# Attention scores from stacked upper and lower parts instead of full float32 products, the mask written by VectorE, and branch B loaded by thirds

## The reference, cut to what matters

```python
xn = rmsnorm(x, g_in);  h = xn @ w_in            # 5648 columns, split into dq dk dv dg gq gk gv gg ga mg
s = einsum('bqhmd,bkhmd->bhmqk', q, k) * DK**-0.5 # 4 heads, 2 maps m, DK = 64
s = where(key_chunk <= q_chunk, s, -inf)          # chunks of 64 frames; the sample group has no mask
p = softmax(s);  a = p[:, :, 0] - lam * p[:, :, 1]
oa = rmsnorm(a @ v) * (1 - lam_init) * silu(da_gate)
ob = rmsnorm(gla(gq, gk, gv, log_a)) * silu(gla_gate)
mixed = sigmoid(g_a) * (oa @ w_branch_a) + sigmoid(g_b) * (ob @ w_branch_b)
y = rmsnorm(x + mixed @ w_out)
```

## Time and profile before

| | |
|---|---|
| median of 3 runs (lowest to highest) | 948.97 us (947.03 to 949.14) |
| profiled execution, its own time | 948.3 us |
| its span, first to last instruction | 946.5 us |
| mean granted TensorE clock | 0.996 |
| PE / PEld / DVE / ACT / POOL busy | 96% / 88% / 51% / 38% / 13% |
| first attention scores, last attention scores | 401.4 us, 757.7 us |

### The profile page before, as it was taken

The page is one execution under the profiler, slowest core; times in us unless marked ns, Lnnn a source line. Parts: engine busy times, 40 slices in busy tenths (PEclk is TensorE's granted clock), DMA queues, the critical chain, the costliest instruction groups (busy, mean ns, idle before and its releaser), DMA issues. The chain is left out here.

```text
span 946.5 us, 16619 instructions
## 1 busy us (share of the span) xinstructions
PE 910.5 (96%) x6648; PEld 831.3 (88%) x6648; DVE 485.8 (51%) x1098; ACT 364.3 (38%) x878; POOL 122.6 (13%) x210
## 2 busy tenths in 40 slices
PE   5899999999999999999999999999998999999997
PEld 4699999989999999999889899898997989988884
DVE  5623377741216776244643464455447676991223
ACT  6645354422335444134443353335334332430010
POOL 2001133210102222000000000000001103540000
PEclk9999999999999999999999999999999999999999
DMA  8022012213110213151032202121123325541222
GB/s 274 2 58 58 23 46 63 76 46 99 45 45 24 68 37 96 52 193 46 24 137 74 74 1 66 54 75 46 46 91 116 91 69 177 175 165 45 89 89 78
DMA packets 85903, 74.11 MB, mean 78 GB/s; under 512 B 4730, under 2 KB 78148, under 8 KB 85572
## 3 DMA queue, kind: packets, MB, share of 16 engines
q1 hardware_dynamic: 85828, 73.06, 25.4%
HBM read 53.32 MB, written 19.73 MB: 77 GB/s over the span
## 5 line engine op out<-in xcount | busy, mean ns | idle before, releaser
L1420 PE MATMUL proj_bank<-x_hi,w_hi 128*128 128x352 f32 x1056 | 350.9, 332 | 2.5 <-DVE w_lo L627 2.5
L1422 PE MATMUL proj_bank<-x_hi,w_lo 128*128 128x352 f32 x1056 | 340.2, 322 | 0.0
L1421 PE MATMUL proj_bank<-x_lo,w_hi 128*128 128x352 f32 x1056 | 339.6, 322 | 0.0
L1420 PEld LDWEIGHTS proj_bank<-x_hi,w_hi 128*128 128x128 f32 x1056 | 199.1, 189 | 4.8 <-DVE w_lo L627 2.8
L1421 PEld LDWEIGHTS proj_bank<-x_lo,w_hi 128*128 128x128 f32 x1056 | 199.6, 189 | 0.0
L1422 PEld LDWEIGHTS proj_bank<-x_hi,w_lo 128*128 128x128 f32 x1056 | 198.9, 188 | 0.0
L627 DVE TENSOR_TENSOR w_lo<-w_raw,w_hi 128x1024 fp32r<-128x1024 f32 x49 | 59.9, 1223 | 69.8 <-ACT w_hi L623 69.8
L994 ACT ACTIVATE probs<-score_banks,softmax_stats 128x128 f32<-128x128 f32 (+8 forms) x72 | 51.2, 713 | 78.1 <-DVE softmax_stats L1336 69.3
L1062 POOL TENSOR_TENSOR stats<-stats,minus_half 128x1 f32<-128x1 f32 (+1 forms) x36 | 22.4, 622 | 371.0 <-DVE stats L1369 371.0
L1047 POOL TENSOR_TENSOR decays<-log_decay 128x128 f32<-128x128 f32 (+1 forms) x122 | 47.6, 425 | 157.7 <-ACT log_decay L931 157.7
L623 ACT ACTIVATE w_hi<-w_raw 128x1024 fp32r<-128x1024 f32 (+1 forms) x53 | 55.1, 1039 | 17.2 <-PE proj_bank L1422 14.5
(11 more groups left out here) (186 smaller groups left out, 1403.3 us busy)
## 6 DMA issues: line engine op xcount, KB each, us to landing
w_raw<-in_w_in SPq DMA_DIRECT2D x44, 512.0 KB, 4.6
merge_tanh_scratch<-feature_stage SPq DMA_DIRECT2D x16, 528.0 KB, 3.1
feature_stage<-merge_tanh_scratch SPq DMA_DIRECT2D x10, 528.0 KB, 3.6
x_rows<-in_x_prompt SPq DMA_DIRECT2D x8, 512.0 KB, 6.5
w_raw<-in_w_out SPq DMA_DIRECT2D x8, 512.0 KB, 4.5
branch_out<-in_x_prompt SPq DMA_DIRECT2D x8, 512.0 KB, 3.7
out<-branch_out SPq DMA_DIRECT2D x8, 512.0 KB, 2.6
tokens_stage<-merge_tanh_scratch SPq DMA_DIRECT2D x6, 528.0 KB, 3.7
```

Source lines behind the costliest of these rows:

```text
L1420: nc.tensor.matmul(out, wh, xh, start=first, stop=False)
L1421: nc.tensor.matmul(out, wh, xl, start=False, stop=False)
L1422: return nc.tensor.matmul(out, wl, xh, start=False, stop=last)
```

## The change

Scores: a key is stored stacked along the contraction. For map m the 128 partitions of `K[:, m, :]` hold the rounded upper part of the key in the map's own 64 partitions and the lower part in the other 64. The stationary operand `QD` has four 128-column planes per step: for each map the upper part of the query twice (both halves of the partitions), and the lower part in the map's own half with zeros in the other. Two fp32r matmuls over all 128 rows then give (q_hi·k_hi + q_hi·k_lo) + q_lo·k_hi. POOL makes both operands: `ks` stacks a third of the keys of a head, `kc` the cached 256, `qd` the queries of the next step; each POOL instruction waits for the one before (`alone`). The mask product goes; DVE overwrites the masked 64 x 64 corner of the scores with -1e30 before the maximum. `dk` units now pass through `FT`, the feature stages, as `dv` does. `OBS` goes: the last tile's x_lo products of a third come first (`ulo`), and branch B's third is then loaded from DRAM straight into BLB and split in place.

```diff
@@ stage_list
-        stages.append(("unit", t, th, 0))
+        if t < len(tiles) - 1:
+            stages.append(("unit", t, th, 0))
+        else:
+            for n in ((0, 1), (), (2,))[th]:
+                stages.append(("ulo", t, n))
+                stages.append(("obload", n))
...
+        if kind == "dk" and i:
+            keys.append(("ks", i, th))
+        elif kind == "dk":
+            stages.append(("ks", i, th))
...
+        if n == 0:
+            stages.append(("qd", 0, 0))
@@ step
         if now:
             stages.append(("aS",) + now)
+        if at_step(s + 1):
+            stages.append(("qd",) + at_step(s + 1))
...
         if two:
             stages.append(("aQ",) + two)
+        stages.extend(keys)
+        keys.clear()
+        if now and now[1] == 1:
+            stages.append(("kc", now[0]))
...
-        if s == NTT:
-            stages.append(("obload",))
@@ SP
                 elif kind == "obload":
-                    sp.wait_ge(s_obst, 16)
-                    sp.dma_start(t_["OBS"]..., ob_dram).then_inc(s_obld, 16)
+                    th = st[1]
...
+                    sp.wait_ge(s_xldone, th + 1)
+                    sp.dma_start(BLB[:, :, cols].bitcast(F), ob_dram...[:, :, cols]).then_inc(s_obld[th], 16)
@@ SP, cload of head h
-                        filled(sp, ("cache", h - 1))
+                        sp.wait_ge(s_kc, h)
@@ GpSimd
+            def alone(ins):
+                alone_no[0] += 1
+                ins.then_inc(s_pwork, 1)
+                pool.wait_ge(s_pwork, alone_no[0])
+            def stack_keys(h, cols, src, s_done):
+                K = t_["K"][h % 2]
+                for m in range(2):
+                    r, other = slice(64 * m, 64 * m + 64), slice(64 - 64 * m, P - 64 * m)
+                    alone(nc.gpsimd.tensor_copy(K[r, m, cols], src[r, :]))
+                    last = nc.gpsimd.tensor_tensor(K[other, m, cols], src[r, :], K[r, m, cols].bitcast(F), ALU.subtract)
+                    if m == 0:
+                        alone(last)
+                last.then_inc(s_done, 1)
...
+                elif st[0] == "qd":
...
+                    if s >= 2:
+                        pool.wait_ge(s_sc, 2 * (s - 1))
...
+                    for m in range(2):
+                        r, other = slice(64 * m, 64 * m + 64), slice(64 - 64 * m, P - 64 * m)
+                        alone(nc.gpsimd.tensor_copy(QD[r, 2 * m, 0:n], Q[r, tok(i)]))
+                        alone(nc.gpsimd.tensor_copy(QD[other, 2 * m, 0:n], Q[r, tok(i)]))
+                        last = nc.gpsimd.tensor_tensor(QD[r, 2 * m + 1, 0:n], Q[r, tok(i)], QD[r, 2 * m, 0:n].bitcast(F),
+                                                       ALU.subtract)
+                        if m == 0:
+                            alone(last)
+                    last.then_inc(s_qd, 1)
@@ VectorE, aS
+                        if i < TT:
+                            w = nk - 64
+                            link(nc.vector.memset(SC[0:64, 2 * m + w // 512, w % 512:w % 512 + 64], BIG))
                         link(nc.vector.reduce_max(...))
@@ TensorE, aS
-                        pe.wait_ge(s_uout, units_done(ft_at["dk", h]))
+                        pe.wait_ge(s_ks, 3 * (h + 1))
...
+                    pe.wait_ge(s_qd, s + 1)
+                    for m in range(2):
+                        if s:
+                            pe.wait_ge(s_ex, 2 * s - 1 + m)
+                        for b in range(-(-nk // 512)):
+                            keys = K[:, m, c0 + 512 * b:c0 + 512 * b + w]
+                            nc.tensor.matmul(out, QD[:, 2 * m, 0:nq], keys, start=True, stop=False)
+                            last = nc.tensor.matmul(out, QD[:, 2 * m + 1, 0:nq], keys, start=False, stop=True)
+                        last.then_inc(s_sc, 1)
```

More of the change, by code:

```diff
@@ L124, in stage_list @@
     stages = []
-    later, branch, carried = [], [], []
+    later, branch, carried, keys = [], [], [], []
     def whole(kind, i):
@@ L315, in hybrid_kernel @@
     NP_ = len(tiles)
-    ft_tiles = [t for t, (k, _, _) in enumerate(tiles) if k not in ("ga", "gk", "gq", "dq", "dk")]
+    ft_tiles = [t for t, (k, _, _) in enumerate(tiles) if k not in ("ga", "gk", "gq", "dq")]
     ft_no = {t: n for n, t in enumerate(ft_tiles)}
@@ L429, in attention @@
             low = dict(
-                GATE=[al(f"da_gate{s}", [P, T]) for s in range(2)], Q1=al("da_q1", [P, T]), K1=al("da_k1", [P, KC]),
+                QD=[al(f"q_stacked{s}", [P, 4, P], R) for s in range(2)],
+                GATE=[al(f"da_gate{s}", [P, T]) for s in range(2)], Q1=al("da_q1", [P, T]), K1=al("k_stacked1", [P, 2, KC], R),
                 V1=al("da_v1", [P, NTT + 2, DV]),
@@ L530, in hybrid_kernel @@
         s_lame = sem("lambda_exp")
-        s_obld = sem("gla_branch_loaded")
+        s_obld = [sem(f"gla_branch_loaded{th}") for th in range(3)]
         s_bh = sem("gla_branch_hi")
@@ L545, in hybrid_kernel @@
         s_gconst = sem("gla_consts_loaded")
-        s_mrld = sem("chunk_mask_loaded")
+        s_pwork = sem("pool_chain")
+        s_ks = sem("k_stacked")
+        s_kc = sem("cache_k_stacked")
+        s_qd = sem("q_stacked")
+        s_xldone = sem("x_lo_thirds_used")
         s_gfin = sem("final_gain_loaded")
@@ L853, in _ @@
                         freed(act, ("aO", i - 2, NTT - 1))
-                    if th == 0 and tk in ("dq", "dk") and i >= 2:
-                        act.wait_ge(s_sc, 2 * NTT * (i - 1))
+                    if th == 0 and tk == "dq" and i >= 2:
+                        act.wait_ge(s_qd, NTT * (i - 1))
                     act.wait_ge(s_unit, u + 1)
@@ L1458, in _ @@
                             pe.wait_ge(s_uout, u - 1)
-                    for k in range(KD_ // 2 * st[3], KD_ // 2 * (st[3] + 1)):
+                    for k in range(KD_ // 2 * st[3] if t < NP_ - 1 else 0, KD_ // 2 * (st[3] + 1)):
+                        if t == NP_ - 1:
+                            nc.tensor.matmul(bank, w_hi[t % 2][:, k, :], XH[:, k, cols], start=False, stop=False)
+                            last = nc.tensor.matmul(bank, w_lo[t % 2][:, k, :], XH[:, k, cols], start=False, stop=k == KD_ - 1)
+                            continue
                         if t < 2:
@@ L1470, in _ @@
                         last.then_inc(s_unit, 1)
+                elif kind == "ulo":
+                    t, th = st[1], st[2]
+                    u = unit_no(t, th)
+                    if th == 0:
+                        pe.wait_ge(s_wlo, t + 1)
+                    pe.wait_ge(s_uout, u - 1)
+                    for k in range(KD_):
+                        last = nc.tensor.matmul(PJ[u % 2][:, 0:TH], w_hi[t % 2][:, k, :], XL[:, k, TH * th:TH * (th + 1)],
+                                                start=k == 0, stop=False)
+                    last.then_inc(s_xldone, 1)
                 elif kind == "bunit":
@@ L1518, in _ @@
                     pe.wait_ge(s_uout, units_done(t))
-                    x = t_["K"][tiles[t][1] % 2] if tiles[t][0] == "dk" else FT[ft_no[t] % NFT]
+                    x = FT[ft_no[t] % NFT]
                     take()
```

99 lines of the change are left out of this document (54 added, 45 removed).

## The result

The change made the kernel slower: 958.62 us median of 4 runs (958.09 to 959.5) against 948.85 us of 4 runs of the kernel before beside it (947.03 to 949.14). The ratio is 1.0108, 95% interval 1.009 to 1.0125. The forecast was 945.5 us with a range up to 953.5. The profiled execution took 959.5 us, its span is 957.7 us against 946.5.

A forecast was written before the change was run, and what follows sets the result against it. It took PE's own stream as the bound: -15 us of scores, +2 swallowed, +7.7 POOL's lateness and +1.8 GLA gave -3.5 us, so 945.5 us from a median of 948.97, range 938 to 953.5.

The forecast's parts named there:

- DVE hides the memsets: DVE in attention: two corner memsets a step, at most some 0.15 us each, hidden except where PE already waits.
- 2 us for all that is swallowed: Attention: charge for PE's saving lost where it already waits for DVE, and for the memsets there.
- The score stream, 15 us: PE's attention scores: 51.6 us old against 37.1 new, saving taken as 15 us, about 0.44 a step at 1024 keys.
- The way out of the old shape: PE, from scores to value matmuls: the array shape change loses 0.10 us, within 0.19 for each of 36 shape changes.
- POOL's lateness, 7.7 us: Attention head changes: PE waits for POOL's key thirds and queries, 5.2 + 1.5 + 1.0 us.
- rival 1: POOL fits: copies priced near the memset, only one head-change place waits, 2.7 us, GLA nothing; 938.7 us; chance 0.2.
- GLA, 1.8 us: GLA part: two thirds of head 0's keys ahead of a power delay DVE's product 2.7 us, 0.8 being slack.
- Branch B, costed at nothing: Branch B's thirds, requested 6.4 us before their split: no cost; a late one costs its lateness once.
- The lock between DVE and POOL: Head changes and GLA: DVE subtractions with both inputs in SBUF hold up POOL, 1.3 or 1.0 us a place.
- rival 2: POOL's queue bounds head changes: copies as dear as subtractions, 18.3 us of waits with GLA, 954.3 us; chance 0.24.
- Rival 3: PE scores: shape change not saved, or fp32r at 128 columns slower than 0.11; saving 8, 952.5 us; chance 0.07.
- rival 4: PE scores: giving up side-by-side halves doubles the scores' 36.2 us; some 985 us; chance 0.01.

The follow-up runs named there:

- e11: Kernel before with DVE's two memsets a step added, its mask product kept: 954.94 us, ratio 1.0071 to the kernel before.
- e5: e4 with branch B loaded early into its own stage, as in the kernel before: 943.01 us, ratio 0.9944 to the kernel before.
- e4: Changed kernel with POOL's stacking work cut to one column and DVE's memsets left out: 945.39 us, ratio 0.9976 to the kernel before.
- e15: e9 without POOL's wait for DVE's da_out_scaled: 946.48 us, ratio 0.9983 to the kernel before.
- e9: e8 with the mask written by an ACT copy instead of DVE's memset: 945.68 us, ratio 0.9973 to the kernel before.
- e8: e6 plus one memset for both maps and branch B's first third loaded earlier: 950.25 us, ratio 1.0018 to the kernel before.
- e6: Changed kernel with queries two steps ahead, key thirds one a step, POOL's stacking held behind DVE's three SBUF-to-SBUF operations: 955.7 us, ratio 1.0071.
- e14: Changed kernel with only the mask changed, an ACT copy instead of DVE's two memsets: 956.43 us, ratio 1.0093 to the kernel before.
- e13: e9 with head 0's second and third key thirds moved behind POOL's subtractions of a GLA chunk: 945.71 us, ratio 0.997.
- e12: Kernel before with branch B loaded by thirds into x_lo's place, last tile's x_lo products first: 949.26 us, ratio 1.0006.
- e2: Changed kernel with DVE's two memsets a step left out: 955.5 us, ratio 1.0079 to the kernel before.

## Why the prediction was wrong

- **DVE hides the memsets: the step that failed.** "Elsewhere DVE is half idle and hides the memsets", with 2 us for all that is swallowed. DVE's idle time lies behind `da_out` in a step; from the start of a step to `da_out` it is one chain, and PE reached the token transposes of the kernel before with no slack to it. A half idle engine was read as slack, where the wait that ends last should have been looked for. e11 measures the memsets alone as 6.7 us, and e5 shows some 6 us swallowed without them. In the ledger PE's new waits for DVE are 9.6 us, or some 11 with what the list leaves out, where the sum had 2.
- **The score stream, 15 us: mis-sized.** 11.2 measured, 9.1 in the stages and 2.1 at the values. The prediction's sum leaves out the last transpose, 0.11 us a step (0.16 where projection stands ahead), or 4.2 in all, that the stages hold; without it the new stages are 40.6 us where 37.1 were foreseen. Steps of 640 to 1024 keys came as priced. The 3.5 us are almost all in the short ones: 2.8 us at i = 0 of the later heads and at i = 8, where nothing is saved at all (1.00 us before and after, 0.90 to 1.22 at i = 8), since the values behind the scores wait for ACT's copy of what PE transposed just ahead, and the longer stage had covered that round trip. The way out of the old shape was charged with 0.10 us in each of the 36 steps and is 2.1 us in all, not 3.6; the old stages were 1.7 us dearer than priced.
- **POOL's lateness, 7.7 us: right in place, near in size.** 3.7 us at (0, 7) for 5.2, 1.2 at (1, 6) for 1.5, at (2, 6) nothing worth a row for 1.0. POOL's prices held; its groups in the attention of after:

```profile
L1137 POOL CAST q_stacked<-da_q 64x128 fp32r<-64x128 f32 x60 | 19.5, 325 | 8.7 <-PE score_banks L1728 4.9
L1075 POOL TENSOR_TENSOR k_stacked<-feature_stage,k_stacked 64x352 fp32r<-64x352 f32 x18 | 17.8, 988 | 1.4
L1074 POOL CAST k_stacked<-feature_stage 64x352 fp32r<-64x352 f32 x18 | 9.4, 522 | 1.2
```

  The copy of 352 columns took 0.52 us on average (0.55 taken), so rival 1's near-memset price was wrong. Undisturbed copies, as in POOL's timeline near (0, 7):

```profile
468.25 0.48 POOL L1074 CAST k_stacked<-feature_stage 64x352 fp32r<-64x352 f32 x1
470.66 0.28 POOL L1137 CAST q_stacked<-da_q 64x128 fp32r<-64x128 f32 x1
474.48 0.20 POOL L1137 CAST q_stacked<-da_q 64x32 fp32r<-64x32 f32 x1
```

  That is about 0.84 ns a column and some 0.18 us besides; a 256-column copy alone takes 0.39 us. In the rate the trace agrees with the "GPSIMD Engine Reference" of the Trainium skill, Engine selection, by which the prediction's estimate was 0.3 to 0.4 us; the estimate left out the fixed part, and so came out low. What was left out is the clock: the wait at (0, 7) is followed by 3.4 us at the 1.2 GHz level, 1.7 us more, so the place costs 5.4.
- **GLA, 1.8 us: right.** 1.4 measured (from a fixed projection matmul to the first score), with PE waiting 0.8 us for `k_decayed_to_end` at 338, against none near 337 in the earlier trace rows.
- **Branch B, costed at nothing: wrong, by less.** The prediction gave it 6.4 us between its request and its split; in e4 ACT could start 6.1 us after the issue at 705.07. But the issue stands in SP's queue behind a load that waits for a store (2.7 to 4.9 us), and behind its late landing stand in turn ACT, DVE with the row maxima, and PE. It was worth 3 us from e4 to e5, 0.6 on the kernel before, with a half-clock stretch behind it in after.
- **The lock between DVE and POOL** was charged for DVE's two-input operations alone. It also stretches DVE's TENSOR_SCALARs from SBUF to SBUF (0.35 to 0.45 us, 0.23 to 0.36 and 0.30 in after), one from 0.35 to 1.08 beside a key subtraction at 465.60, while the one that reads PSUM keeps its 0.35. "SBUF — State Buffer" of the Trainium skill, Who interferes with whom, says that a tensor_scalar can enter a two-port mode, where its operands allow it, and then contends with POOL; the trace agrees in that all three are stretched and the one that reads PSUM is not, and the prediction should have used it. Which of the three run in that mode no run shows. PE feels about 1 us of it (e15 against e9).
- **The rivals.** The other side came, but by no rival's mechanism: rival 2 asked for POOL copies of 0.72 us and got 0.52. Rival 3's size, a saving of 8 us, was about as far off as the forecast's 15, and its mechanism is excluded by the 0.03 us from transpose to score and by the steps of 640 keys, with their fp32r passes of 128 columns, which came as priced; rival 4 is excluded by the 1.96 us of the scores.

What stays open: how the time from a store into the scratch to the load that waits for it comes about (2.7 to 4.9 us in the profiled runs; 6.0 to 7.3 in e8 and the runs built on it, where a load of branch B was issued just ahead of the store). It may be what spreads the times of e6 and e14, but only profiled executions show it.

## What to carry to other kernels

A busy share says nothing about slack: before an operation is put on a half idle engine, follow its queue from the event that starts it to the one that the bound engine waits for, and ask what the bound engine, once faster, will run into. Here 11 us saved on PE met chains on DVE, POOL, ACT and SP that had been cut to PE's old pace, and each repair alone moved the wait to the next one; only together (e9, e13) did they pay, 2.6 to 2.8 us. The same work is free in another place: 0.28 us on ACT inside a wait beat 0.11 us on DVE inside a chain.

## What the runs showed of the hardware beyond that

- A PE wait can cost more than its length: behind 3.7 us of waiting (busy 0.34 of 4 us) the granted clock was 0.50 for 3.4 us; around 4.7 us in e14 for 6.8 us; behind 1.9 us of waiting at (3, 4) for 3.4 us. It need not: at the same place the clock stayed at 1.00 behind 2.1 us in e12 and behind 2.9 us in e2, and was 0.50 for 6.8 us around 2.8 us in e4. The length of the wait alone does not decide; what does stays open.
- A 64 x 64 memset of 0.11 us on DVE costs 0.24 us where the operation behind it depended on nothing before, since a maximum that had started under its predecessor's end must now wait for the memset's.
- Going from transposes to fp32r matmuls over all rows costs no drain: the first score starts 0.03 us after the last transpose (0.20 before for a half-row matmul) and takes 0.32 us instead of 0.23, together 0.35 where two full cadences are 0.34.
